# The second block's attention in the first one's form, weight loads issued earlier, and unread products ahead of waits

## What is computed

```python
# forgetting attention, 8 heads of 64; cum is the running sum of log forget gates
logits = einsum('bhqd,bhkd->bhqk', qb, kf) + cb[..., :, None] - cum[:, :, None, :]
logits = where(pos[None, :] <= pb[:, None], logits, NEG_INF)
p = softmax(logits); o = einsum('bhqk,bhkd->bhqd', p, vf)
...
# experts of either block
for e in range(N_EXPERTS_2):
    h = silu(xt @ w_gate[e]) * (xt @ w_up[e])
    y = y + combine[:, e:e + 1] * (h @ w_down[e])
```

## Time and profile before

| | us |
|---|---|
| median of 3 runs | 1913.36 (1911.27 to 1916.16) |
| the profiled execution | 1914.55 |
| its span | 1912.7 |
| TensorE busy | 1652.7 (86%) |
| VectorE / ScalarE / GpSimd busy | 503.5 / 328.6 / 376.9 |
| chain that ended last | TensorE 53%, DMA 30%, VectorE 7%, GpSimd 4% |

### The profile page before, as it was taken

One profiled execution on the slowest core, in us unless ns is written; L12 is line 12 of the kernel. 1 busy time (PEld: TensorE's weight loads), 2 busy tenths in 40 slices (PEclk: granted clock), 3 DMA queues, 4 the chain that ended last, 5 costly groups with the idle time before them and its releaser, 6 DMA issues.

```text
span 1912.7 us, 18683 instructions
## 1 busy us (share of the span) xinstructions
PE 1652.7 (86%) x7098; PEld 807.8 (42%) x7098; DVE 503.5 (26%) x1203; ACT 328.6 (17%) x718; POOL 376.9 (20%) x360
## 2 busy tenths in 40 slices
PE   8999989989897887778777759999999997988775
PEld 4445456444544332222222225546644444544332
DVE  4565664110324301000000022513300015311110
ACT  3002541121311000000000020313300012111111
POOL 0122544881201111111110110020001001222222
PEclk9999999989997999989899969999999997998898
DMA  9123004412645999999999674940031245999993
GB/s 315 41 88 110 1 12 174 177 45 99 219 178 216 421 414 419 416 421 415 417 418 415 251 233 113 244 110 23 1 88 61 71 160 224 401 398 403 401 402 123
DMA packets 101718, 436.96 MB, mean 228 GB/s; under 512 B 15656, under 2 KB 23496, under 8 KB 75392
## 3 DMA queue, kind: packets, MB, share of 16 engines
q1 hardware_dynamic: 58896, 299.03, 41.0%
q10 hardware_dynamic: 24272, 105.99, 13.5%
q0 software_dynamic: 18464, 30.76, 6.1%
HBM read 414.19 MB, written 40.91 MB: 238 GB/s over the span
## 4 chain that ended last, share of the span: by engine, by line
PE 53%; DMA 30%; DVE 7%; POOL 4%; ACT 3%; issue 2%; SPq 1%; ACTq 0%; POOLq 0%; DVEq 0%
PE ps L261 27%; DMA ring<-in_w 19%; DMA ring<-in_w_expert_up 9%; PE ps L1763 8%; PE ps L1346 5%; PE ps L1779 2%; PE ps L2244 2%; DMA work<-hmid,rowtok 1%; PE ps L773 1%; PE ps L758 1%; SPq L1942 1%; PE ps L1372 1%; PE ps L732 1%; POOL ring L1106 1%; POOL ring L1107 1%
## 5 line engine op out<-in xcount | busy, mean ns | idle before, releaser
L1763 PE MATMUL ps<-ring,work 128*64 128x256 f32 (+1 forms) x1472 | 273.3, 529 | 74.3 <-DMA ring<-in_w 44.3
L261 PE MATMUL ps<-kept,ring 128*128 128x512 f32 x640 | 280.5, 598 | 2.9 <-DVE kept L1401 1.3
L1763 PEld LDWEIGHTS ps<-ring,work 128*64 128x64 f32 x1472 | 113.3, 150 | 238.3 <-issue 119.9
L261 PEld LDWEIGHTS ps<-kept,ring 128*128 128x128 f32 x640 | 122.2, 192 | 156.9 <-issue 153.9
L1881 DVE TENSOR_TENSOR work<-work,ps 128x256 f32<-128x256 f32 (+1 forms) x64 | 22.7, 354 | 629.0 <-ACT work L1840 608.2
L1779 PE MATMUL ps<-ring,work 128*64 128x512 f32 x544 | 129.5, 611 | 27.2 <-issue 26.2
L1763 PE MATMUL ps<-kept,work 128*64 128x512 f32 (+1 forms) x640 | 117.6, 524 | 30.4 <-DMA kept<-in_w 18.0
L1927 POOL DMA_INDIRECT hres<-work,rowdst x33 | 51.7, 1567 | 434.0 <-ACT work L1850 433.7
L261 PE MATMUL ps<-ring,kept 128*128 128x512 f32 (+1 forms) x320 | 124.7, 550 | 0.3 <-PE ps L261 0.3
L1346 PE MATMUL ps<-ring,kept 128*128 128x512 f32 x256 | 114.5, 602 | 1.7 <-ACTq L245 1.4
L1840 ACT ACTIVATE work<-ps 128x256 f32<-128x256 f32 (+1 forms) x64 | 21.1, 330 | 458.4 <-PE ps L1763 458.4
(11 more groups left out here) (453 smaller groups left out, 1876.9 us busy)
## 6 DMA issues: line engine op xcount, KB each, us to landing
ring<-in_w SPq DMA_DIRECT2D x46, 2048.0 KB, 29.6
kept<-in_w SPq DMA_DIRECT2D x21, 2048.0 KB, 29.7
ring<-in_w ACTq DMA_DIRECT2D x20, 2048.0 KB, 23.0
ring<-in_w_in SPq DMA_DIRECT2D x13, 2048.0 KB, 14.4
ring<-in_w_expert_gate SPq DMA_DIRECT2D x24, 1024.0 KB, 34.4
ring<-in_w_expert_up SPq DMA_DIRECT2D x24, 1024.0 KB, 41.1
kept<-in_w ACTq DMA_DIRECT2D x9, 2048.0 KB, 25.6
ring<-in_w_expert_down ACTq DMA_DIRECT2D x18, 1024.0 KB, 30.2
```

The lines of the kernel that those rows point to most:

```text
L261: last = nc.tensor.matmul(out_, l, r, start=i == 0, stop=i == len(pairs) - 1)
L1763: last = nc.tensor.matmul(ps[64 * hf:64 * hf + 64, bank, 0:ff].rearrange("p (w n) -> p w n", w=2), xT[:, k, :], up[:, :, k * ff + hf * hw: ...
```

## The change

In the second block's attention the mask is added to the bias by GpSimd (`fox_pool`), the probabilities are scaled before the turn by GpSimd (token tiles 0 and 1) or ScalarE (2 and 3), and the product with the values takes the first block's form, over the causal part only. The first scores are issued ahead of the last value projection, the first gate's four products are placed at the end of the loop, and `o2` with its turn goes away. `moe_sp` waits for the logits, the turned rows and the stored rows instead of the first gather, and issues expert 2's up weights earlier in the second block. A new helper, `keep_busy`, issues products of 512 columns that nobody reads: one in front of each wait for up weights from the first reused place on, five in front of the first gathered turn, two in front of the last turn of each norm, and twelve at the second block's entry. The order of a few VectorE steps changes, the overflow's first gather is issued four experts earlier, and the slots in every second block of 16 are numbered backwards. Semaphores are renamed to match; buffers move. The core of the diff (new lines of changed functions, with removed ones where they carry work):

```diff
+        def keep_busy(bank, n):
+
+            for _ in range(n):
+                nc.tensor.matmul(ps[:, bank, :].rearrange("p (a n) -> p a n", a=4), ident[:, :],
+                                 ident[:, :].unsqueeze(1).to_broadcast([P, 4, P]), start=True, stop=True)
...
             def turn(t):
-                pe.wait_ge(S(f"{n}_xn"), since(f"{n}_xn") + t + 1)
-                pe.wait_ge(S(f"{n}_xa"), since(f"{n}_xa") + t + 1)
                 if t >= 2:
                     pe.wait_ge(S(f"{n}_hd"), since(f"{n}_hd") + t - 1)
                     pe.wait_ge(S(f"{n}_ha"), since(f"{n}_ha") + t - 1)
+                if t == 3:
+                    keep_busy(2, 2)
+                pe.wait_ge(S(f"{n}_xn"), since(f"{n}_xn") + t + 1)
+                pe.wait_ge(S(f"{n}_xa"), since(f"{n}_xa") + t + 1)
                 turn_rows(t).then_inc(S(f"{n}_turned"), 1)
...
             if m:
                 logits(2)
-                lsum(2)
             turn(3)
             if m:
+                lsum(2)
                 logits(3)
                 lsum(3)
...
+            turned_dve(n, 3, gain)
             if m:
                 choose_dve(m, 2, 0)
-            turned_dve(n, 3, gain)
-            if m:
                 choose_dve(m, 2, 1)
...
+            keep_busy(0, 5)
             turn(0)
...
                     g = 2 * (i % places)
-                    pe.wait_ge(S(f"w{m}_{g}"), since(f"w{m}_{g}") + 32 * (i // places + 1))
                     n("xready", i // 2 + 1)
                     if i >= 2:
                         n("hready", i - 1)
+                    if i >= places:
+                        keep_busy(i % 2, 1)
+                    pe.wait_ge(S(f"w{m}_{g}"), since(f"w{m}_{g}") + 32 * (i // places + 1))
...
-                if e == NE - 4:
+                if e == NE - 8:
                     pool.wait_ge(S(f"planned{m}"), since(f"planned{m}") + 1)
                     pool.wait_ge(S(f"xturned{m}"), since(f"xturned{m}") + NE // 2 - 3)
                     over_gather(pool, m, rowtok[:, NE // 2:NE // 2 + 1])
+                if e == NE - 4:
                     add_rows(pool, m, rowdst[:, NE + NOV:NE + NOV + 1], yb[:, 0, :]).then_inc(S(f"over{m}_store"), 16)
...
                 for e in range(2):
                     load_up(e)
                     load_down(e)
+                load_up(2)
                 sp.wait_ge(S("w_used1"), since("w_used1") + 21)
-                for e in range(2, 4):
-                    load_up(e)
-                    load_down(e)
-            sp.wait_ge(S(f"xg{m}_0"), since(f"xg{m}_0") + 16)
+                load_down(2)
+                load_up(3)
+                load_down(3)
+            sp.wait_ge(S(f"logits{m}"), since(f"logits{m}") + T)
+            sp.wait_ge(S(f"n{m}_turned"), since(f"n{m}_turned") + T)
+            sp.wait_ge(S(f"hmid{m}"), since(f"hmid{m}") + 16 * T)
             for e in range(places * 2 // 3, places):
                 load_up(e)
                 if places == 3:
...
+            keep_busy(4, 8)
+            pe.wait_ge(S("xback_0"), since("xback_0") + 16)
+            keep_busy(4, 4)
             for t in range(T):
...
             variances(1)
+            gained(3)
+            scale(1)
             turned(0)
-            scale(1)
-            gained(3)
             variances(2)
+            scale(2)
             turned(1)
-            scale(2)
             variances(3)
+            scale(3)
             turned(2)
-            scale(3)
             turned(3)
 
...
+                if t == T - 1:
+                    for eng in ("act", "dve"):
+                        pe.wait_ge(S(f"fox_placed_{eng}"), 4)
+                    fox_scores(pe, 0)
+                    fox_scores(pe, 2)
...
+        def fox_scores(pe, i):
+            if i >= 4:
+                pe.wait_ge(S("f2_masked"), since("f2_masked") + i - 2)
+            for m in range(2):
+                h, t = head1(i + m)
+                r = slice(64 * m, 64 * m + 64)
+                n = (t + 1) * P
+                nc.tensor.matmul(ps[:, (i + m) % 4, 0:n], q2[r, h // 2, t * P:t * P + P], k2[r, h // 2, 0:n],
+                                 start=True, stop=True).then_inc(S("f2_scores"), 1)
...
-                    for m in range(2):
-                        n = (head1(i)[1] + 1) * P
-                        nc.tensor.matmul(ps[:, (i + m) % 4, n - P:n], ident[:, :], causal, start=False, stop=True
-                                         ).then_inc(S("f2_scores"), 1)
...
+            for i in range(2, N2 + 6):
+                j = i - 4
                 if 0 <= j < N2:
                     if j == 0:
+                        pe.wait_ge(S("fox_out"), since("fox_out") + 11)
+                        pe.wait_ge(S("fox_sum"), since("fox_sum") + 12)
+                        pe.sem_inc(S("w_used1"), 1)
+                    if by_pool(j):
+                        pe.wait_ge(S("f2_norm_pool"), pool_count(j) + 1)
+                    else:
+                        pe.wait_ge(S("f2_norm"), j - pool_count(j) + 1)
                     if j >= 2:
                         pe.wait_ge(S("f2_pT"), since("f2_pT") + j - 1)
+                    for c in range(head1(j)[1] + 1):
+                        last = nc.tensor.transpose(ps[:, 4 + j % 2, c * P:c * P + P], prf(j)[:, c * P:c * P + P],
                                                    ident[:, :])
                     last.then_inc(S("f2_turned"), 1)
+                if i % 2 == 0 and i + 2 < N2:
+                    fox_scores(pe, i + 2)
+                if i in (N2 + 1, N2 + 4):
+                    mix_first(pe, (i - N2) // 4)
+                if i == 13:
+                    pe.wait_ge(S("fox_out"), since("fox_out") + 12)
+                if i >= 13 and (i - 13) % 8 == 0:
+                    hp = (i - 13) // 8
+                    pe.wait_ge(S("f2_pT"), since("f2_pT") + 8 * hp + 8)
+                    if hp >= 2:
+                        pe.wait_ge(S("f2_out"), since("f2_out") + hp - 1)
+                    for c in range(T):
+                        for m in range(2):
+                            last = nc.tensor.matmul(ps[64 * m:64 * m + 64, 6 + hp % 2, c * P:SEQ],
+                                                    v2[:, c, (2 * hp + m) * 64:(2 * hp + m) * 64 + 64],
+                                                    pTf(hp, m)[:, 512 * c:384 * c + 512], start=c == 0, stop=c == T - 1)
+                    last.then_inc(S("f2_pv"), 1)
+            for i in (2, 3):
+                mix_first(pe, i)
...
-        def turn_o2(pe):
-            pe.wait_ge(S("f2_out"), since("f2_out") + N2)
-            for f in range(4):
-                for t in range(T):
-                    last = nc.tensor.transpose(ps[:, 4 + f, t * P:t * P + P], o2[:, t, f * P:f * P + P], ident[:, :])
-                last.then_inc(S("f2_oturned"), 1)
...
+        def fox_pool(pool):
+            def build(hp, m):
+                nc.gpsimd.tensor_tensor(bias2(hp, m).rearrange("p (t n) -> p t n", t=T),
+                                        Fb[:, 2 * hp + m, :].rearrange("p (t n) -> p t n", t=T),
+                                        causal.unsqueeze(1).to_broadcast([P, T, P]), ALU.add).then_inc(S("f2_bias"), 1)
+            pool.wait_ge(S("F_in"), 16)
+            pool.wait_ge(S("causal_in"), 16)
+            pool.wait_ge(S("glu_done"), NU)
+            for hp in range(2):
+                for m in range(2):
+                    build(hp, m)
+            for hp in range(H2 // 2):
+                for k in range(8):
+                    i, t, m = 8 * hp + k, k // 2, k % 2
+                    pool.wait_ge(S("f2_masked"), since("f2_masked") + i + 1)
+                    if t < T - 1:
+                        nc.gpsimd.tensor_copy(bias2(hp, m)[:, t * P:t * P + P], Fb[:, 2 * hp + m, t * P:t * P + P]
+                                              ).then_inc(S("f2_bias"), 1)
+                    elif hp + 2 < H2 // 2:
+                        build(hp + 2, m)
+                    j = i - 1
+                    if k and by_pool(j):
+                        n = (j % 8 // 2 + 1) * P
+                        pool.wait_ge(S("f2_rden"), since("f2_rden") + j + 1)
+                        nc.gpsimd.tensor_scalar(prf(j)[:, 0:n], prf(j)[:, 0:n], rden[:, j:j + 1], None, ALU.mult
+                                                ).then_inc(S("f2_norm_pool"), 1)
 
...
+                j = i - 1
+                if 0 <= j < N2:
+                    dve.wait_ge(S("f2_probs"), since("f2_probs") + j + 1)
+                    dve.reciprocal(rden[:, j:j + 1], den[:, j:j + 1]).then_inc(S("f2_rden"), 1)
+                j = i - 5
+                if 0 <= j < N2:
+                    hp, t, m = j // 8, j % 8 // 2, j % 2
                     dve.wait_ge(S("f2_turned"), since("f2_turned") + j + 1)
+                    if hp >= 2 and j % 8 == 0:
+                        dve.wait_ge(S("f2_pv"), since("f2_pv") + hp - 1)
```

(23 more changed lines are left out.)

107 lines of the change are left out of this document (36 added, 71 removed).

## The result

The changed kernel takes 1902.67 us (median of 8 runs, 1900.43 to 1907.11) where the kernel before takes 1914.26 us beside it. The ratio is 0.9941, interval 0.9925 to 0.9957: 11.6 us faster. The forecast was 1879 us, range 1862 to 1897. The direction was right, the size three times too large, and the range missed it. The profiled execution spans 1900.8 us (1912.7 before).

The account below looks back on a forecast made before the run. Full DMA engines bound the expert stages, TensorE or its chain through VectorE and ScalarE the rest. Terms 10 + 7 + 7 + 2.6 + 2.3 + 1.5 + 4 = 34.4 off 1914.55, 1.2 less for the median: 1879 us, range 1862 to 1897.

Parts of the forecast that it names:

- up to the first expert stage: Cross attention's first 32 products: two unread products ahead of the last turn shorten the clock's pause, 2.3 us gained.
- first entry, stage and tail: First expert stage: 7 us from earlier third-expert loads and a sooner queue restart, 1.3 from a faster last up product.
- entry of the second block and u projection: Second block's entry: twelve products make the first turn 5 us late, faster turns and warm projection repay; 1.5 us gained.
- attention: Second block's attention: mask off TensorE, paired value products, 11.2 us a pair of heads set by VectorE; 10 us gained.
- from the gates to the end: Second expert stage: 7 us from earlier weight loads at its entry, 1.3 from a faster last up product.
- slot order: Expert stages: backward numbering evens gathered rows over DMA engines, 4 us gained; bounds 0 to 16 and some 6.
- rival A: Both expert entries: weights in flight delay the router's gathers, head start given back, both gain nothing; 1893 us, chance 0.12.
- Rival E: Unread products don't hold the clock: 2.3 + 2.6 us and 3 of each entry go; 1890 us, chance 0.06.
- rival B: Second block's attention: GpSimd sets the pace, a pair at 12.7 or 15.3 us; 1884 or 1895 us, chance 0.13.
- Products ahead of up waits: Expert stages: 29 and 26 unread products hide in TensorE's waits, cost nothing; last up product gains 1.3 us a stage.
- D: Up waits: all 55 unread products land on the path, 47 us slower; 1926 us, chance 0.04.
- C: Slot order evens the DMA engines, 10 to 14 us more gained; 1867 us, chance 0.15.

Follow-up runs that it names:

- e9: e7 with, in the second expert stage, expert 4's down and expert 5's up weights also waiting for the first gather; ratio to the kernel before 0.9861.
- e12: The kernel before with only the earlier weight loads at both entries to the expert stages; ratio to the kernel before 0.9953.
- e7: Changed kernel without the twelve products, plain slots, only one of the third expert's three loads ahead of the first stage's first gather; ratio to the kernel before 0.9857.
- e2: Changed kernel with the wait for the first gather put back in both expert stages; ratio to the kernel before 0.9949.
- e11: The kernel before with only the two unread products ahead of each norm's last turn, and the logits sum moved behind that turn; ratio to the kernel before 0.9956.
- e10: e7 with GpSimd scaling three of four token tiles of each pair of heads in the attention; ratio to the kernel before 0.9852.

## Why the prediction missed

| term | forecast | lead gained in the trace |
|---|---|---|
| up to the first expert stage | -2.3 | -6.1 |
| first entry, stage and tail | -8.3 | +0.5 |
| entry of the second block and u projection | -1.5 | +5.0 |
| state space part and projections | 0 | +2.0 |
| attention | -10 | -8.1 |
| from the gates to the end | -8.3 | -5.2 |
| slot order | -4 | in none of these |
| sum | -34.4 | -11.9 |

*First entry: the step that failed.* The term of 7 us for this entry stood on the step that the queue restarts 7.5 us sooner, at a first up product that ends near 615.5, with the gather as long as before. I gave the delayed gather to rival A, as a case of its own with a chance of 0.12. But with two of the three loads released early, the loads that make the head start are the ones that stand in front of the gather. The gather cost 4.0 us, the clock 2.8, and the next load hung on both: the product ended at 617.2 although TensorE had arrived 6.1 us sooner, and the entry gave 0 of its 7 us. The 1.2 us that the order of VectorE's steps was to save don't show either: the gather is issued 6.2 us sooner, at a lead of 6.1. Rival A was right for this entry. At the second the gather was delayed too (7.62 us for 5.00), but there it cost little: six places hold enough work, as I read it, e9 finds nothing in a sooner gather, and e12 shows 5.6 of the 7. What I should have asked of the timeline is when the queue runs dry: 10 us of weights ahead, restart only after the product, so all that the head start buys beyond the restart's own gain is idle time later. e7 shows that 5 of the 7 us were to be had (from 7.2 to 11.9).

*Entry of the second block.* The step "TensorE starts them near 1117 and ends near 1129" was in the frame of the kernel before, in which x arrives 5.6 us later. In the new frame that is 1111.4 to 1123.4; they ran from 1114.10 to 1126.7. I had not looked at what TensorE's sequencer does between the stages. And I let the loss of 5 us be made good by warm turns and a warm projection. Three of the turns were warm; the projection was not, and takes 30 us with twelve, three or no products. The step that failed here is that the twelve would hold the clock up to the projection. The bound "3 lost" was too small by 2.

*Up to the first stage.* More came than forecast: 2.9 us in the query projection, where 2.3 were forecast, 1.0 at the last turn ahead of the router, which I had not counted, and 2.2 already at 407, 1.6 of them where the kernel before has a fall of the clock (384 to 388 us) and the changed one has none. The last is chance: e2 has that fall again.

*The clock.* Rival E was right at two of its places (the first up product, 9.93 us; the last one, 8.78) and wrong at one, the cross attention, where the pair did what it should, 27.70 us. The difference is what follows: there the pause behind the products is 1.11 us, here it is 3.23 us. So the slow first up product was the gather's doing as well: in e2, with the wait back, the pause is 0.29 us and the product takes 7.09. In the state space part the changed kernel has a fall of the clock that the one before has not in its profile, at the same work (windows, first before, then after):

```profile
1190.00:1205.00 15.00, 11.28 (x101) 9.18 (x101) 14.20 (x22) 2.78 (x4) 0.00 (x0) 1.00 0.94 248
```

```profile
1190.00:1205.00 15.00, 12.11 (x84) 8.38 (x84) 13.60 (x21) 1.17 (x2) 0.00 (x0) 0.77 0.81 213
```

It costs 2.0 us (the lead goes from -0.6 to +1.4 at 1304). The fall is 6.8 us long here, and e11 and e12, which change nothing in this part, have one of 3.4 us at this place, so it isn't bound to a change of this part; why it comes stays open.

*Attention.* The count by engines held: 2.37 us for a product with the values, 11.06 to 11.36 us for a pair, and from 1320 to 1358 us VectorE ends 8.1 of the 8.8 us that TensorE waits. Of the 1.9 us that are missing, 1.3 are the pair with the low clock. GpSimd was hidden, rival B is refuted by e10. What I had as a reserve for ScalarE was a real part of the pair.

*Products ahead of up waits.* They cost nothing, as said, and D did not come about there. It came about at the one place where products stood ahead of no wait of that length. Their gain of 1.3 us a stage did not show.

*From the gates to the end.* The gain is 5.8 us from 1550 to 1850, and 0.6 are lost behind it. The earlier weight loads of the second entry are 4.4 of it by e2 (1.4 us gained there with the wait back), against 7 forecast.

*Slot order.* My 4 us rested on a difference of rates (415 to 429 GB/s) between a short window and a long one, which shows no cause. C is refuted. The Trainium skill's rule ("DMA: Bandwidth & Descriptors", The descriptor swizzle), by which the sum was 4 us smaller, gave the better number; that the gathers follow it is not shown by this.

*The chances.* A, D and E were given as cases that exclude each other; they came together, each at one place, and so the time lies above A's 1893 and E's 1890; that the first stage arrived 3.8 us better than forecast, in part by chance, hides some of the miss. With one range around each case alone, 1902.7 was in no case but the far end of D.

## What to carry to other kernels

Bytes sent early gain only what the next load in line can also start earlier: find what the reload waits for, and count the time for which the queue will be dry. The short transfer that the critical path needed next waited behind the large ones in flight, so size the head start to end before it is issued. Products that only keep the clock up paid here ahead of a pause of 1.1 us, did not hold it over one of 3.2 us, and cost 7 us where twelve of them, 12.6 us long, stood in a pause of which some 4 us were left; look in the sequencer's records for when they can start at all.

## What the runs showed of the hardware that I had not expected

- A short write behind weights in flight is held back first, and then slowed as well: the write of x to DRAM was issued at 595.92, and its first packet started at 600.06, 4.1 us later, when 241 of the 256 pieces of weights in flight had started; in the kernel before it was 0.83 us (602.12 to 602.95). From the first packet to the last it then took 4.2 us, against 2.0. The gather's packets follow the write's in both. In the prediction I read the Trainium skill ("DMA: Bandwidth & Descriptors", Queues, rings and completion order) as speaking for "slowed, not blocked". The page says that an engine changes between queues only at packet boundaries, after some 9 to 17 descriptors. One piece of 16 KB of these weights occupies an engine for 0.6 us (the median of the 256; 53 of them end in 2 us on 16 engines), so an estimate by that page is 5 to 10 us for a turn. A wait of 4.1 us fits into one such turn, so the page's rule and the trace agree, and my reading was wrong. A queue served strictly in the order of issue is less likely: in the full stretches the gathers land in 14.3 us in the median, where SyncE's 2 MB loads take 29.6 (page, part 6). No run here tests it.
- Between the first block's experts and the second block TensorE's sequencer is held for 5 us by 41 semaphore clears (one every 0.12 us), in which no product is issued.
- The u projection behind the pause takes 29.5 to 30.7 us in every kernel of this study, with the granted clock low ahead of it and into it: for 27 to 31 us in one piece, or, with twelve or three unread products in the pause, in two pieces of 10 to 14 us with the full clock between. Work ahead of it moved the low stretch and did not shorten the projection.
